# Inverse softmax sums spread into rows by transposing a repeated column, in both attentions of a two-block kernel

## What is computed

```python
# sparse attention, for a block of 128 queries (first block)
    sc = jnp.where(valid[:, :, None, :], sc, -jnp.inf)
    p = jax.nn.softmax(sc, axis=-1).astype(v.dtype)
    return jnp.einsum('bthk,btkd->bthd', p, v_sel)
...
    y_b = jax.nn.silu(z_b) * sparse_attention(q, k, val, q_idx, k_idx, w_idx)

# dense attention, for a block of 128 queries (second block)
    s = jnp.einsum('bkgqd,bksd->bkgqs', qi, k).astype(jnp.float32) * scale
    pr = jax.nn.softmax(s, axis=-1).astype(v.dtype)
    return jnp.einsum('bkgqs,bksd->bkgqd', pr, v)
```

## Time and profile before

| what | value |
|---|---|
| time, median of 3 runs | 3312.0 us |
| lowest and highest of the 3 | 3308.2 and 3312.25 us |
| the profiled execution's own time | 3307.63 us |
| its span, first to last instruction | 3305.8 us |
| PE busy | 3046.1 us, 92% |
| DVE busy | 2085.4 us, 63% |
| ACT busy | 1402.9 us, 42% |
| POOL busy | 1165.6 us, 35% |
| sparse attention, layer 0 | about 423 to 584 us of the span |
| sparse attention, layer 1 | about 1055 to 1216 us |
| dense attention | about 1509 to 1758 us |

### The profile page before, as it was taken

The page is one execution under the profiler, slowest core; times in us unless marked ns, Lnnn a source line. Parts: engine busy times, 40 slices in busy tenths (PEclk is TensorE's granted clock), DMA queues, the critical chain, the costliest instruction groups (busy, mean ns, idle before and its releaser), DMA issues. The chain is left out here.

```text
span 3305.8 us, 44327 instructions
## 1 busy us (share of the span) xinstructions
PE 3046.1 (92%) x16273; PEld 2492.3 (75%) x16273; DVE 2085.4 (63%) x3778; ACT 1402.9 (42%) x2758; POOL 1165.6 (35%) x1251
## 2 busy tenths in 40 slices
PE   5899989989999999798999999998889898999999
PEld 3578867756787667587887887788877788788777
DVE  7899965687997757676772014678857687211343
ACT  2366466234763751335663211455434553221231
POOL 2237421331562225421004242244543444424331
PEclk9999999999999999899999999999999899999999
DMA  6322334531234244410002114123231332412431
GB/s 237 115 73 80 109 112 121 190 131 34 80 99 140 90 147 134 123 39 1 1 11 93 48 55 142 40 62 89 68 116 48 75 86 73 159 48 103 152 105 39
DMA packets 228314, 303.14 MB, mean 92 GB/s; under 512 B 41055, under 2 KB 142175, under 8 KB 225921
## 3 DMA queue, kind: packets, MB, share of 16 engines
q1 hardware_dynamic: 216578, 279.33, 28.0%
q10 hardware_dynamic: 11520, 20.98, 1.7%
HBM read 241.91 MB, written 58.33 MB: 91 GB/s over the span
## 5 line engine op out<-in xcount | busy, mean ns | idle before, releaser
L877 PE MATMUL psum<-qs,hT 128*128 128x512 f32 x1344 | 308.5, 391 | 6.6 <-POOL qs L962 6.1
L877 PEld LDWEIGHTS psum<-qs,hT 128*128 128x128 f32 x1344 | 252.7, 189 | 62.4 <-issue 5.3
L2583 PE MATMUL psum<-bhsn,bringn 128*128 128x512 f32 x1056 | 241.0, 389 | 2.4 <-DVE bhsn L2665 1.5
L2583 PE MATMUL psum<-bhsa,bringa 128*128 128x512 f32 x1056 | 240.1, 389 | 3.1 <-POOL bringa L2644 3.1
L2583 PEld LDWEIGHTS psum<-bhsn,bringn 128*128 128x128 f32 x1056 | 197.9, 188 | 45.0 <-DVE bmixn L2705 2.2
L2583 PEld LDWEIGHTS psum<-bhsa,bringa 128*128 128x128 f32 x1056 | 198.1, 188 | 44.6 <-issue 3.5
L2962 PE MATMUL psum<-hTs,cws 128*128 128x512 f32 x960 | 229.3, 395 | 0.0
L2962 PEld LDWEIGHTS psum<-hTs,cws 128*128 128x128 f32 x960 | 178.9, 189 | 36.2
L1709 PE MATMUL psum<-w_out,oys 128*128 128x512 f32 x768 | 181.1, 398 | 9.4 <-POOL oys L1782 4.8
L1042 DVE TENSOR_SCALAR_CACHE_REDUCE junk<-score,cand 128x384 uint8<-128x384 f32 x248 | 186.8, 810 | 2.2
L1709 PEld LDWEIGHTS psum<-w_out,oys 128*128 128x128 f32 x768 | 146.5, 192 | 44.0 <-POOL oys L1782 7.1
(11 more groups left out here) (557 smaller groups left out, 7162.6 us busy)
## 6 DMA issues: line engine op xcount, KB each, us to landing
stg<-in_w_in SPq DMA_DIRECT2D x96, 256.0 KB, 2.7
score<-in_w_ada SPq DMA_DIRECT2D x32, 512.0 KB, 4.2
pj<-ptmp ACTq DMA_DIRECT2D x64, 256.0 KB, 2.2
dlb<-blocks SPq DMA_DIRECT2D x32, 512.0 KB
dlb<-in_w_in SPq DMA_DIRECT2D x20, 512.0 KB, 4.0
wa<-in_w_ada SPq DMA_DIRECT2D x8, 1024.0 KB, 10.6
ostg<-in_w_out SPq DMA_DIRECT2D x16, 512.0 KB, 6.0
x<-ozb SPq DMA_DIRECT2D x16, 512.0 KB, 3.0
```

Source lines behind the costliest of these rows:

```text
L877: mm = pe.matmul(bank(m), lhs, rhs, start=(kc == 0 and x == 0), stop=(kc == KC - 1 and x == 2))
L2583: mm = pe.matmul(ps[:, m, :], w[:, a, fs], h, start=(j == 0 and x == 0), stop=(j == KC - 1 and x == 2))
```

## The change

In the dense attention the four matmuls become four transposes of the same repeated column. In the sparse attention, the buffer `ri` goes (a pad of its size stays, so that the buffers behind it keep their places), and a new buffer `riw` of 4 x 64 columns takes the inverses. DVE writes each inverse 64 times: the reciprocal reads the sum 64 times and writes 256 elements per partition. PE then turns two heads at once, 128 columns, with one transpose: two transposes in place of four matmuls. As `riw` is a single buffer, the reciprocal of a group waits for the transposes of the group before it, on a new semaphore `s_row`. No instruction changes its place in any engine's order.

```diff
-        ri = k.sb(ctx, f"ri_{l}", [P, N])
+        k.sb(ctx, f"ri_pad_{l}", [P, N])
...
+        riw = k.sb(ctx, f"riw_{l}", [P, GH, HD])
...
                 for j in range(GH // 2):
-                    for b in range(2):
-                        hd = GH * v + 2 * j + b
-                        pe.matmul(ps[HD * b:HD * (b + 1), 6, ROWS + j * P:ROWS + (j + 1) * P],
-                                  ri[:, hd:hd + 1].to_broadcast([P, HD]), ident, start=True, stop=True)
+                    mm = pe.transpose(ps[:, 6, ROWS + j * P:ROWS + (j + 1) * P],
+                                      riw[:, 2 * j:2 * j + 2, :].rearrange("p b d -> p (b d)"), ident)
+                mm.then_inc(s_row, 1)
...
             def invert(v):
                 dve.wait_ge(s_exp, GH * (v + 1))
-                dve.reciprocal(ri[:, GH * v:GH * (v + 1)], rs[:, GH * v:GH * (v + 1)]).then_inc(s_ri, 1)
+                if v:
+                    dve.wait_ge(s_row, v)
+                dve.reciprocal(riw[:, :, :], bc(rs[:, GH * v:GH * (v + 1)], 2, HD)).then_inc(s_ri, 1)
...
                 for j in range(G):
-                    mm = pe.matmul(ps[:, 6 + (m + 1) % 2, j * P:(j + 1) * P],
-                                   ri[:, G * m + j:G * m + j + 1].to_broadcast([P, P]), k.cst[:, C_ID:C_ID + P],
-                                   start=True, stop=True)
+                    mm = pe.transpose(ps[:, 6 + (m + 1) % 2, j * P:(j + 1) * P],
+                                      ri[:, G * m + j:G * m + j + 1].to_broadcast([P, P]), k.cst[:, C_ID:C_ID + P])
```

More of the change, by code:

```diff
@@ L1142, in stage_attend @@
             "z_times_values", "y_b", "dve_chain"))
-        s_in, s_hi, s_lo, s_mv, s_rstd, s_vc, s_vg, s_vn, s_uz, s_wm, s_mix, s_pow = (k.sem(n) for n in (
+        s_in, s_hi, s_lo, s_mv, s_rstd, s_vc, s_vg, s_vn, s_uz, s_wm, s_mix, s_pow, s_row = (k.sem(n) for n in (
             "inputs", "q_hi", "q_lo", "mean_var", "rstd", "v_centred", "v_scaled", "v_normed", "u_times_z", "w_masked",
-            "mixed", "power"))
+            "mixed", "power", "inverse_rows"))
         s_q = [k.sem(f"q_loaded{i}") for i in range(2)]
```

## The result

| | median | runs | ratio to before, 95% interval |
|---|---|---|---|
| kernel before | 3308.4 us | 20 (3303.9 to 3315.8) | |
| kernel after | 3314.0 us | 20 (3307.0 to 3321.7) | 1.0017 (1.0011 to 1.0024) |

The change costs 5.6 us. The forecast was 10.2 us less than before; the measured time lies above the range. The time after also spreads more than the one before, 15 us from lowest to highest against 12.

The account below looks back on a forecast made before the run. PE was taken to bound the dense and late sparse attention, DVE's work to count in the early sparse part. Dense -7.2 and sparse 2 x (-4.3 + 2.8) = -3.0 made -10.2 us: 3301.8 us, range 3295 to 3313.

Parts of the forecast that it names:

- What of x lies on the path?: Sparse attention, DVE: 2.8 us a layer of the longer reciprocals passes on, in groups 2 to 5; later ones hidden.
- x: Sparse attention, DVE: extra time of the 256-element reciprocal over the 172 ns of the 4-element one, taken as 1.05 us.
- Dense attention: Four transposes for four matmuls on PE save 0.45 us in each of 16 groups, 7.2 us, all of it counting.
- The reciprocal: Sparse attention, DVE: 256 elements take 1.2 us, from about 153 ns fixed and 3.5 to 4.8 ns per element.
- rival 2: Sparse reciprocal at 6 to 9 ns per element, x = 1.6 to 2.1; sum -5.8 to +0.2 us, middle 3309; chance 0.22.
- rival 3: DVE becomes the bound of the whole sparse attention; at x = 3 sum +13.4 us, 3325 us; chance 0.1.
- the formula: Early sparse groups: (x - 0.44) + x + (2x - 1) us a layer reaches the path.
- PE's prices in the sparse attention: Two transposes for four matmuls save 0.28 us a group, 0.6 in group 0; 4.3 us a layer, groups 3 and 4 uncounted.
- Rival 4: Sparse group 0: fewer matmuls put PE's clock rise off by up to 4 us; sum -6.2, 3305.8 us; chance 0.06.
- The new wait: Sparse attention: the reciprocal's wait for the previous group's transposes is real only in group 15; priced at nothing.
- Rivals 1 and 5: Sparse reciprocal at one element per cycle, 3296.8 us, chance 0.25; and transposes no cheaper than matmuls, 3309 us, chance 0.02.

Follow-up runs that it names:

- DVE's part alone: Kernel before plus the 256-element reciprocal into the repeated buffer; PE keeps its four f32 matmuls, dense attention unchanged: 1.0039 and 1.0053 of before.
- the copy on ACT: Full change, but DVE's reciprocal takes 4 elements and ACT repeats it 64 times: 0.9974 and 0.9977 of before; only the sparse attention changed so: 1.0005.
- copy on DVE: Full change, but DVE takes the reciprocal of 4 elements and repeats it with a plain copy: 0.9981 of the kernel before.
- the sparse part alone: Full change with the dense attention's edit undone: 1.0053 and 1.0051 of the kernel before, 16.8 and 16.3 us above.

## Why the prediction was wrong

**The step that failed** is "What of x lies on the path?", 2.8 us a layer, and within it the later groups, of which it says "so I take 1 us as hidden there" and adds nothing. DVE's part alone makes the stage 5.5 to 9.8 us longer. Some 3 us of that lie in the groups from 5 on, where the sum had nothing, and 4 to 7 in the early ones. The price of the reciprocal, which goes into that step, was too small as well.

**Dense attention: right.** 0.45 us a group were forecast, 0.47 came (15.48 to 15.01), 7.7 us in the stage for 7.2. Alone it makes the kernel 4 to 5 us faster.

**The reciprocal: its size was wrong.** "I take the middle, 1.2 us" went by a fixed part of 153 ns, that of another operation. It is 142 ns, and an element costs 6.3 ns, so 1.75 us: rival 2's "fixed part of 137 to 145 ns, 8 to 16 less than I took". One row of 4 elements gave a slope that hung on 11 ns of the fixed part, and 256 elements multiplied it. In the forecast's own terms x is then 1.58 for 1.05, which passes on 4.9 us a layer and makes a sum of about -6 us: still a gain. So the price alone doesn't turn the sign. That the long reciprocal is the cause of the loss all the same is shown from both sides: it alone makes the loss, and with the copy in its place the loss is gone.

The Trainium skill (VectorE: DVE Perf Modes, First, the fixed hardware budget) names an iterative divide with a repeat count of 8; the estimate of 2.1 us made from it was nearer to the measured 1.75 than my 1.2. The trace doesn't agree with 8 cycles an element: 6.3 ns are about 6 cycles of its 0.96 GHz.

**What of it lies on the path: too little.** In the early groups the formula's 4.9 us for x = 1.58 is about what came (4 to 7). In the later ones the pauses didn't cover 1.58 us: the gate came late in groups 5, 7, 9 and 10 as well, by 0.58 to 1.23 us. The prediction was at odds with itself here. It took 1 us as hidden, and yet its rival 2 put nothing on the later groups at x = 1.6, and its rival 3 took 1.5 to 2 us as covered. The sign turns when the missing terms are added up, which is an estimate: -6 us for the right price of the reciprocal, 2 x 3 us for the later groups, and 2 x 1.3 us for what of PE's gain doesn't arrive in their 8 steps (next paragraph) make +2.6. The rest to +5.6 is less than the early groups vary by.

**PE's prices in the sparse attention: right, the sum made of them too large.** A spreading costs 0.27 us less, as forecast. The 4.3 us a layer needed all of it to arrive in groups 5 to 15. Where PE waits for nobody it nearly does: the steps from groups 10, 11 and 12 take 13.0, 12.1 and 9.3 us with the transposes and 13.2, 12.3 and 9.5 with the matmuls, at the same long reciprocal. In the steps that end in a wait for the gate 0.1 us arrives at most, and in the 8 later steps together it is 0.9 of 2.2 us. The stretch of 540 to 560 us, with PE busy for 20.00 of 20 us, was right for itself and not for all the groups from 5 on. With the copy on ACT the stage is 1 to 3 us shorter than before, but there ACT's extra work takes some of the gain back, and how much isn't shown.

**Rival 4, the clock: the mechanism is real, the place was wrong.** I looked for it in the transposes in place of matmuls in group 0. It comes with PE's longer waits for the gate: it fell behind waits of 1.67 and 2.07 us, and with the matmuls kept as well (DVE's part alone: 12.3 and 12.4 us from group 4 in its second timing, behind waits of 2.4 us, for 10.6 without a fall). Where one step can be seen with and without a fall and with the same work, it costs 1.1 to 2.5 us (10.8, 12.0 and 12.2 for 9.7, 10.6 for 9.0, 12.3 and 12.4 for 10.6), and nothing in the step from group 3. A long wait doesn't always bring it: the same kernel fell behind a wait of 2.42 us in layer 1 and not behind 2.43 in layer 0 (copy on DVE). In which executions it falls, and why, stays open. That it falls in some only is in line with the wider spread after: of the 20 executions the three with the highest granted clock (0.972 on the whole) took 3307.0, 3309.6 and 3309.6 us, the two with the lowest (0.966) 3319.3 and 3321.65. In group 0 the clock of the full change does rise later, about 2.3 us behind the start of the spreading for 1.2 before, and the step takes 7.6 us. But with the matmuls kept it rises 2.0 and 2.5 us behind (layer 0, 7.9 and 8.1 us), and the sparse part alone, with the same transposes, takes 6.7. So the transposes aren't what puts it off.

**The new wait: as forecast.** It is real in group 15 alone, where the timeline of DVE shows it, and nobody but the last gate stands behind it:

```profile
587.89 1.75 DVE L1493 RECIPROCAL riw<-rs 128x256 f32<-128x256 f32 x1 [1.40 <-PE psum L1332]
```

Rivals 1 and 5 fell (1747 ns, and 0.09 us for each of four transposes). Rival 1's reason, that every large f32 instruction runs at one element per cycle, didn't hold in its own rows either: the product of 512 elements at 474.99 took 1.25 us, 2.4 ns an element, against 421 ns for 256. Rival 3 named the right kind of failure, DVE as the bound also in late groups. Its price was to be reached from 2.3 us extra; by its own terms, (x - 0.44) + 2x - 1 + x and 1 us more, the 7.9 us are reached at 2.1. The loss came at 1.58.

## What to carry to other kernels

Price a vector operation at a new size by rows of the same operation at two sizes. If there is only a short one, say that the price is unknown, for it says almost nothing about the slope. Then ask of every wait that is taken as hidden whether it is longer than the work added, group by group. Keep the expensive operation small, and repeat its result with a plain copy. Where two engines are near their bound together, only part of what one is spared arrives, while much of what the other gets in addition does, and a wait that grows may bring the clock down on top.

## What the hardware showed that was not expected

- The reciprocal on DVE costs 6.3 ns more for each further element (167 ns for 4, 1747 ns for 256), against 421 ns for a product and 348 ns for a plain copy of 256 elements.
- PE's granted clock went to 0.50 after single waits of 1.67 to 2.4 us in some executions and layers, and stayed at 1.00 after the same waits in others. With the fall the step from group 2 took 10.6 us in place of 9.0; the step from group 3 took 9.7 either way.
- A transposed 128-column product leaves one record, and the f32 matmul of the same operands two, at the same 0.09 to 0.10 us each.
